# Two prompt tiles loaded channel-major, in an eight-core streaming encoder layer

## The chip, the cores and the metric

The kernel runs on one Trainium2 chip, as one program on all 8 cores, with no exchange between them. The time is the device time of the slowest core in microseconds (us). A core has the engines PE (TensorE: matmuls, and transposes as matmuls), DVE (VectorE), ACT (ScalarE), POOL (GpSimd) and SP (SyncE, which here only starts DMAs). POOL and ACT start DMAs too.

## What is computed

One encoder layer for two groups of rows. The work is split so that each core has 2048 prompt rows (four tiles of 512 rows) and 32 rows of running streams ("sample rows"). Each sub-layer is `x + rmsnorm(f(rmsnorm(x)))`:

```
proj = rmsnorm(x) @ w_in                      # 1024 -> 2048: u | B | C | h, 512 each
y_pool = per group of 128: mean over a trailing window (2, 4, 8, 16) - u, @ w_pool, * scale
y_conv = B * conv3(C * h)                     # causal, depthwise
x = x + rmsnorm(concat(norm_g(y_pool), norm_g(y_conv)) @ w_out)
k, v = rmsnorm(mem) @ w_k, rmsnorm(mem) @ w_v # 256 memory rows; sample rows: cached k, v
x = x + rmsnorm(softmax(rmsnorm(x) @ w_q @ k.T / 16) @ v @ w_co)      # 4 heads of 256
x = x + rmsnorm(relu(rmsnorm(x) @ w_up) ** 2 @ w_down)                # 4096 hidden
rmsnorm(x) = x * rsqrt(mean(x * x, over 1024 channels) + eps) * gain
```

## The kernel before

Matmuls run in bf16 with f32 sums. The contraction index must lie on the partitions, so every projection wants its input channel-major: `xT[0]` and `xT[1]` hold eight slices (`kc`) of 128 channels by 512 rows. The residual `X` is kept row-major, 128 rows by 1024 channels a block, four blocks a tile.

`pre_sub` (line 798) makes a part of `xT` from one block: ACT squares it and sums (`ss`), `rstd` takes `Ln` and `Exp`, `scale_rows` scales the rows into the bf16 buffer `xs` (on DVE or ACT), PE transposes eight 128x128 pieces, and DVE multiplies them from PSUM by the gain, 1024 columns at once. `pre_tile` does that for the four blocks of a tile. Tile 0 is an exception: it is loaded channel-major as f32 (`xt0`) and normed by another path.

The stages, in the order of the program: mixer projections of tiles 0 and 1 (`pool_group`, `conv_group`), `mix_out(0)` and `mix_out(1)` (`out_tile` with `wout`: 16 matmuls of 512 columns for each block), the mixer of tiles 2 and 3 with the four kv blocks (`kv_block`: keys and values of the memory, 16 matmuls each, weights in `wkv`), the fold of keys and values into `Am` and `Bm` (`fold_a`, `fold_b`), attention for all tiles, and the MLP tile by tile. In the MLP `w_up` is streamed in eight blocks through the three buffers `up`, and `w_down` lies in the eight buffers `wdn`, the last four of which are requested when block 7 of `up` has landed. The sample rows go along: `smp_q` (their queries) and `up_smp` (their hidden units) use the weights as the stationary side, with 32 columns moving; `out_smp` uses 32 columns of the sample rows as the stationary side, with 256 weight columns moving and four column groups of the array.

Nothing of this order is written out by hand. Every operation goes into a list with its reads and writes, `Prog.add` finds its dependencies (a tracker of rectangles in SBUF), and `Prog.schedule` replays the list with costs (`c_act`, `c_dve`, `DMA_GBS`, `DMA_FIX`) and takes, for each engine, the ready operation that stands earliest in the program. What comes out is a fixed order for each engine; on the chip each engine goes through its own in order and waits at semaphores. A DMA that POOL starts thus holds up what follows on POOL until its buffer is free. Loads from POOL's queue can convert f32 to bf16; `X` blocks are stored and loaded by SP, which also takes its entries in order.

Of the kernel before, what the change touches and what calls it, by code (L numbers as in the profile page):

```python
# [15 lines left out]
D = 1024  # L16
TP = 2048
# [178 lines left out]
class Prog:  # L196
# [9 lines left out]
    def add(self, opts, reads=(), writes=(), nbytes=0, lead=0, after=None, desc=4096):  # L206

        op = Op()
        op.idx = len(self.ops)
        op.opts = opts  # L210
        op.is_dma = nbytes > 0
        op.bytes = nbytes
        op.desc = desc
        op.deps = {} if after is None else {after: "raw"}
        op.prio = op.idx - lead
        op.ps_new = []
        op.ps_acc = set()
        op.eng = None
        self.ops.append(op)
        multi = len(opts) > 1  # L220
        eng = None if (op.is_dma or multi) else opts[0][0]

        def dep(p, kind):
            if p is not None and p is not op and op.deps.get(p) != "raw":
                op.deps[p] = kind
        for ap in list(reads) + list(writes):
            if isinstance(ap, PV):
                op.ps_acc.add(ap.ps)
                if ap.ps.id not in self.ps_seen:
# [12 lines left out]
        for ap in writes:
            sp, rects = rects_of(ap)
            for r in rects:
                for rec in list(self.tr.find(sp, r)):
                    dep(rec.writer, "war")
                    for rd in rec.readers:
                        dep(rd, "war")
                    q = rec.rect
                    if r[0] <= q[0] and r[1] >= q[1] and r[2] <= q[2] and r[3] >= q[3]:  # L250
                        rec.dead = True
                self.tr.put(sp, r, op)
        return op


    LAT = {("pe", "x"): 0.33, ("x", "pe"): 0.45, ("x", "x"): 0.16, ("s", "s"): 0.10}
    DMA_GBS = {2048: 280.0, 4096: 330.0, 8192: 340.0, 12288: 345.0, 16384: 345.0}
    DMA_FIX = 2.6

    def schedule(self):  # L260
# [14 lines left out]
            if op.ndep == 0:  # L275
                release(op)

        free = {e: 3.5 if e == "pool" else 0.6 for e in self.ENGS}
        hold = {e: 0.0 for e in self.ENGS}
        bank_free = [0.0] * 8  # L280
        bank_busy = [None] * 8
# [3 lines left out]
            for ps in op.ps_acc:  # L285
                ps_left[ps] = ps_left.get(ps, 0) + 1
        dq = {e: [] for e in self.ENGS}
        dq_t = [0.0]

        def dma_next():  # L290
            act = [e for e in self.ENGS if dq[e]]
# [243 lines left out]
def build_program():  # L535
# [4 lines left out]
    def din(name, shape):  # L540
        return nc.dram_tensor(name, list(shape), F32, kind="ExternalInput")
# [1 line left out]
    def dout(name, shape):  # L543
        return nc.dram_tensor(name, list(shape), F32, kind="ExternalOutput")

    xp = din("xp", [TP, D]); xt0 = din("xt0", [4, 128, 1024]); xe = din("xe", [NX, D])
    spool = din("spool", [32, 512]); sconv = din("sconv", [4, 512])
    ckT = din("ckT", [8, 128, 512]); cv = din("cv", [8, 128, 512]); mem = din("mem", [256, D])
    consts = din("consts", [128, 248])
# [2 lines left out]
    gd = {n: din(n, [1, D]) for n in gnames}  # L552
    win_d = din("w_in", [7, 128, 4096])
    wout_d = din("w_out", [128, 8192]); wco_d = din("w_co", [128, 8192])
    wk_d = din("w_k", [16, 128, 512]); wv_d = din("w_v", [16, 128, 512])
    wq_d = din("w_q", [16, 128, 512]); wqT_d = din("w_qT", [16, 128, 512])
    wup_d = din("w_up", [8, 128, 4096]); wdn_d = din("w_down", [8, 128, 4096])
    wpool_d = din("w_pool", [128, 512])
# [76 lines left out]
    sq = rot("sq", 2, TN, BF16)  # L635
    rf = rot("rf", 2, TN)
    mT = rot("mT", 1, 8 * 256, BF16)[0]
    W0 = roff[0]
    assert W0 >= A0 + 106 * K
    wkv = [at("wkv%d" % i, W0 + i * 8192, 4096, BF16) for i in range(2)]  # L640
# [127 lines left out]
        return st[0:r, a:a + n]  # L768


    load(cst[:, :], consts[:, :], 126976, q="act")
    memset(epsb[:, :], EPS)
    act(stat(128), epsb[:, 0:1], AF.Square)
    copy(idb[:, :], idf[:, :])
# [483 lines left out]
    def attn_head(t, hh):  # L1258
# [16 lines left out]
            tt(p2, p2, r.unsqueeze(1).to_broadcast([128, 2, TN]), ALU.mult)  # L1275
        return finish

    def smp_loads():
        wload(kTs[:, :], ckT, 0, 8)
        wload(vSs[:, :], cv, 0, 8)  # L1280

    def smp_q():
        ps = PS(1)
        for j in range(8):
            for kc in range(8):
                mm(ps.v(0, 128, j * NS, (j + 1) * NS), wqk(j, kc), xTek(0, NS)(kc), kc == 0, kc == 7)
# [53 lines left out]
    def up_smp(k, ps):  # L1340
        s = up_slot[(0, k)]
        for jj in range(4):
            c = k * 4 + jj
            cl = c % 16
# [75 lines left out]
    out_smp(lambda kc: mgs[:, kc * NS:(kc + 1) * NS], 8, wo)  # L1420
    pre_tile(2, 0, xT[0])
    mix_out(1)
    for t in range(2, NT):
        for g in range(4):
            step(pool_group(t, g))
            if t == 2:
                kv_done = kv_block(g)
                if g == 0:
                    ext_state_out(kv_done)
                if g < 2:  # L1430
                    kv_loads(g + 2)
# [12 lines left out]
        mix_out(t)
# [176 lines left out]
```

How the kernel before makes its waits and increments, by code:

```python
        def run(e, eng):  # L474
            seen = {}
            ends = sorted(dma_last.items(), key=lambda kv: kv[1].end)
            for n, op in enumerate(seqs[e]):
                if e == "sp" and n == len(seqs[e]) - 1:
                    for k, last in ends:
                        if last.end < op.start - SETTLED and seen.get(k, 0) < last.semval:
                            eng.wait_ge(dsem[k], last.semval)
                            seen[k] = last.semval
                waits = {}
                for p in plan[op]:
                    k, v = (p.sem, p.semval) if p.is_dma else (p.eng, p.sigval)
                    if seen.get(k, 0) >= v:
                        continue
                    if waits.get(k, 0) < v:
                        waits[k] = v
                for k, v in waits.items():
                    eng.wait_ge(dsem[k] if isinstance(k, tuple) else esem[k], v)
                    seen[k] = v
                ins = op.fn(eng, lambda x: x.resolve(psum) if isinstance(x, PV) else x)
                if op.is_dma:
                    ins.then_inc(dsem[op.sem], 16)
                elif op.needs_signal:
                    ins.then_inc(esem[e], 1)
            if e == "sp":
                for k, last in ends:
                    if seen.get(k, 0) < last.semval:
                        eng.wait_ge(dsem[k], last.semval)
```

## Time and profile before

| what | value |
|---|---|
| time, median of 3 runs | 848.71 us (848.17 to 849.42) |
| time of the profiled execution | 848.66 us |
| span of its slowest core (core 6) | 847.1 us |
| PE busy | 813.7 us, 4708 matmuls |
| DVE, ACT, POOL busy | 391.1, 390.8, 102.2 us |
| moved by DMA | 102.39 MB |

The span runs from the first to the last instruction of the slowest core; 1.6 us of the execution lie outside it. The page also has a line with the clock that TensorE was granted in 40 slices; all of them are 9 (90% or more of 2.4 GHz). Matmuls are pipelined: a matmul of 512 columns shows as 0.38 us, but the next one starts 0.22 us after it.

### The profile page before, as it was taken

How to read it: one execution, taken by the hardware profiler on the slowest of the kernel's cores; microseconds unless marked ns; L12 is line 12 of the kernel's file. 1: busy time of each engine (PE TensorE's matmuls, PEld its weight loads, DVE VectorE, ACT ScalarE, POOL GpSimd, SP SyncE). 2: the span in 40 equal slices, each digit the busy share in tenths (PEclk: the TensorE clock that was granted, in tenths of full speed). 3: DMA queues.
4: the chain of work that ended last, by engine and by line, in shares of the span. 5: the costliest groups of instructions: out<-in, count | busy, mean ns of one | idle time of the engine just before them, and what ended most of it. 6: DMA issues, size and time to landing. Idle time of an engine off the chain costs nothing.

```text
span 847.1 us, 13900 instructions; the slowest of 8 cores (841.2 to 847.1 us)
## 1 busy us (share of the span) xinstructions
PE 813.7 (96%) x4708; PEld 391.2 (46%) x4708; DVE 391.1 (46%) x540; ACT 390.8 (46%) x806; POOL 102.2 (12%) x179
## 2 busy tenths in 40 slices
PE   3889999899999999999999999999999999999997
PEld 1444454444644454455454454444444444444443
DVE  4886885568966666765222222241222321222112
ACT  3586786758867556675332233332233411233101
POOL 7612103002111113110010000000000000000000
PEclk9999999999999999999999999999999999999999
DMA  9999439550396606993889716881248820185011
GB/s 196 199 229 202 129 117 208 111 81 1 65 149 113 199 26 187 161 174 84 149 144 165 186 72 132 154 147 53 99 96 156 156 68 26 50 150 100 1 50 50
DMA packets 29793, 102.39 MB, mean 121 GB/s; under 512 B 2386, under 2 KB 13266, under 8 KB 24348
## 3 DMA queue, kind: packets, MB, share of 16 engines
q0 software_dynamic: 19408, 67.32, 46.4%
q1 hardware_dynamic: 9740, 32.75, 11.5%
q10 hardware_dynamic: 576, 1.44, 0.5%
q8 instruction: 39, 0.64, 0.3%
q14 instruction: 30, 0.25, 0.1%
HBM read 144.38 MB, written 18.07 MB: 192 GB/s over the span
## 4 chain that ended last, share of the span: by engine, by line
PE 83%; DMA 11%; DVE 2%; issue 2%; POOL 1%; ACT 1%; another core or an unknown queue 0%; DVEq 0%; ACTq 0%; POOLq 0%
PE ps L670 80%; DMA X<-xp 4%; DMA wdn<-w_down 4%; PE ps L675 2%; DMA wkv<-w_v 2%; DMA up<-w_up 1%; POOL win L744 0%; DVE X L725 0%; ACT junk L699 0%; POOL wdn L744 0%; DVE O L706 0%; DVE z L725 0%; DVE z L706 0%; DVE V L706 0%
## 5 line engine op out<-in xcount | busy, mean ns | idle before, releaser
L670 PE MATMUL ps<-wdn,hid 128*128 128x512 bf16 x1024 | 222.3, 379 | 0.7 <-DMA wdn<-w_down 0.7
L670 PE MATMUL ps<-xT,up 128*128 128x512 bf16 x1024 | 222.6, 379 | 0.0
L670 PEld LDWEIGHTS ps<-wdn,hid 128*128 128x128 bf16 x1024 | 99.9, 98 | 120.4 <-issue 1.2
L670 PEld LDWEIGHTS ps<-xT,up 128*128 128x128 bf16 x1024 | 99.7, 98 | 119.1 <-issue 0.2
L706 DVE TENSOR_TENSOR O<-ps,gp 128x1024 f32<-128x1024 f32 (+1 forms) x49 | 58.3, 1200 | 191.0 <-PE ps L670 122.0
L699 ACT ACTIVATE rt<-ps 128x512 bf16<-128x512 f32 x128 | 76.4, 597 | 142.2 <-PE ps L670 138.3
L670 PE MATMUL ps<-xT,win 128*128 128x512 bf16 x512 | 122.1, 384 | 13.5 <-DMA win<-w_in 12.6
L706 DVE TENSOR_TENSOR hid<-rt 128x512 bf16<-128x512 bf16 x128 | 54.4, 425 | 157.8 <-ACT rt L699 156.0
L699 ACT ACTIVATE sqj<-ps 128x1024 bf16<-128x1024 f32 (+1 forms) x33 | 32.8, 994 | 173.2 <-PE ps L670 171.0
L670 PEld LDWEIGHTS ps<-xT,win 128*128 128x128 bf16 x512 | 49.4, 98 | 71.6 <-issue 17.7
L725 DVE SCALAR_TENSOR_TENSOR X<-O,st,X 128x1024 f32<-128x1024 f32 (+1 forms) x49 | 62.8, 1294 | 4.6 <-DVE O L706 3.8
L744 POOL DMA_DIRECT2D up<-w_up x32 | 17.2, 539 | 378.5 <-PE ps L670 364.9
L706 DVE TENSOR_TENSOR xT<-ps,cst 128x1024 bf16<-128x1024 bf16 x44 | 53.1, 1219 | 20.4 <-PE ps L675 20.2
L670 PE MATMUL ps<-wout,mg 128*128 128x512 bf16 x256 | 58.1, 379 | 3.3 <-DMA wout<-w_out 2.6
L699 ACT ACTIVATE xs<-X 128x1024 bf16<-128x1024 f32 x40 | 41.9, 1050 | 35.4 <-DMA X<-x 31.7
L670 PE MATMUL ps<-xT,Am 128*128 128x512 bf16 x256 | 58.3, 379 | 0.0
L670 PE MATMUL ps<-Bm,mg 128*128 128x512 bf16 x256 | 58.2, 379 | 0.0
L670 PEld LDWEIGHTS ps<-wout,mg 128*128 128x128 bf16 x256 | 24.6, 98 | 31.7 <-issue 3.9
L670 PEld LDWEIGHTS ps<-xT,Am 128*128 128x128 bf16 x256 | 24.2, 98 | 28.5 <-issue 1.7
L670 PEld LDWEIGHTS ps<-Bm,mg 128*128 128x128 bf16 x256 | 24.1, 98 | 27.2 <-issue 0.8
L708 POOL TENSOR_TENSOR psm<-mg 128x512 fp32r<-128x512 bf16 x16 | 19.3, 1208 | 108.8 <-ACT st L699 69.5
L675 PEld LDWEIGHTS ps<-idb,xs 128*128 128x128 bf16 (+1 forms) x412 | 26.2, 98 | 10.2 <-issue 2.0
(184 smaller groups left out, 687.1 us busy)
## 6 DMA issues: line engine op xcount, KB each, us to landing
up<-w_up POOLq DMA_DIRECT2D x32, 1024.0 KB, 9.9
x<-X SPq DMA_DIRECT2D x16, 512.0 KB, 4.2
X<-x SPq DMA_DIRECT2D x16, 512.0 KB, 4.5
wdn<-w_down POOLq DMA_DIRECT2D x8, 1024.0 KB, 30.0
yp<-X SPq DMA_DIRECT2D x15, 512.0 KB, 2.7
X<-xp POOLq DMA_DIRECT2D x8, 512.0 KB, 44.5
X<-xp SPq DMA_DIRECT2D x8, 512.0 KB, 4.4
win<-w_in POOLq DMA_DIRECT2D x4, 768.0 KB, 26.9
```

What stands on the lines that cost most here:

```text
L670: P.add([("pe", lambda e, L: e.matmul(L(out), lhsT=lhsT, rhs=rhs, start=start, stop=stop, skip_group_check=True), max(0.03, n * 0.000421 + ...
L675: P.add([("pe", lambda e, L: e.transpose(out=L(out), in_=in_, identity=idn), 0.065 if in_.dtype == BF16 else 0.25)], reads=[in_, idn], wri ...
L699: return e.activation(out=L(out), in_=L(in_), func=func, scale=scale, **kw)
L706: opts.append(("dve", lambda e, L: e.tensor_tensor(out=L(out), in0=L(in0), in1=L(in1), op=op), c_dve(n, per)))
L708: opts.append(("pool", lambda e, L: e.tensor_tensor(out=L(out), in0=L(in0), in1=L(in1), op=op), 0.18 + n * 0.00168))
L725: return P.add([("dve", lambda e, L: e.scalar_tensor_tensor(out=L(out), in0=L(in0), scalar=scalar, in1=L(in1), op0=op0, op1=op1), c_dve(nc ...
L744: return P.add([(q, lambda e, L: e.dma_start(out=out, in_=in_), 0.5 + nbytes / desc * 0.0005 if q == "pool" else 0.43)], reads=[in_] if rd ...
```

## The change

1. Tiles 2 and 3 of the prompt come a second time, channel-major (`xt23`), and are loaded by POOL's queue straight into `xT` as bf16, one transfer of 2 MB (f32) each. The row-major blocks are still loaded, for the residual and the square sums. `pre_turned` norms `xT` in place: the square sums of the four blocks give four columns of row factors, `rb` splits them into three bf16 parts, POOL multiplies the identity by them (`dg`, three times 512 columns), three matmuls with a matrix of ones turn that into a PSUM tile in which every partition has the 512 row factors, and DVE multiplies the eight slices by gain and factors. No transposes, no `scale_rows` for these two tiles.
2. `w_k` and `w_v` are laid out so that one load reads 16 KB pieces instead of 2 KB pieces.
3. `smp_q` and `up_smp` take the form of `out_smp`: 32 matmuls and 128 matmuls of 256 columns. The result is row-major and `turn_blocks` brings it back with two transposes. `up_smp` now works on two blocks of `up` at once.
4. The scheduler's transfer model has other figures (`DMA_GBS`, start times), and a write that covers an earlier record of the tracker only in part now cuts that record. Both change only which order comes out.

```diff
-                    if r[0] <= q[0] and r[1] >= q[1] and r[2] <= q[2] and r[3] >= q[3]:
+                    if r[0] <= q[0] and r[1] >= q[1] and (sp[0] == "S" or r[2] <= q[2] and r[3] >= q[3]):
                         rec.dead = True
+                        for lo, hi in ((q[2], r[2]), (r[3], q[3])):
+                            if lo < hi:
+                                self.tr.put(sp, (q[0], q[1], lo, hi), rec.writer).readers.update(rec.readers)
...
-    DMA_GBS = {2048: 280.0, 4096: 330.0, 8192: 340.0, 12288: 345.0, 16384: 345.0}
+    DMA_GBS = {1024: 150.0, 2048: 275.0, 4096: 310.0, 8192: 325.0, 12288: 325.0, 16384: 328.0}
...
-        free = {e: 3.5 if e == "pool" else 0.6 for e in self.ENGS}
+        free = {e: 6.9 if e == "pool" else 1.0 for e in self.ENGS}
...
-        dq_t = [0.0]
+        dq_t = [2.6]
...
+    def load_turned(t):
+        load(xT[t % 2][:, :], xt23[t - 2], 2097152, q="pool", desc=16384)
+
+    def pre_turned(t):
+        n = NSUB
+        ss, ln, rs, rem = (stat(128, n) for _ in range(4))
+        for i in range(n):
+            act(xsr[xs_n[0] % 2][:, :], Xof[(t, i)], AF.Square, accum=ss[:, i:i + 1])
+            xs_n[0] += 1
+        act(ln, ss, AF.Ln, scale=1.0 / D, bias=epsb[:, 0:1])
+        act(rs, ln, AF.Exp, scale=-0.5)
+        left = rs
+        for q in range(3):
+            b = rb[:, q * n:(q + 1) * n]
+            copy(b, left)
+            if q < 2:
+                tt(rem, left, b, ALU.subtract)
+                left = rem
+        tt(r3(dg[:, :], 3 * n), idb[:, :].unsqueeze(1).to_broadcast([128, 3 * n, 128]),
+           rb[:, :].unsqueeze(2).to_broadcast([128, 3 * n, 128]), ALU.mult, eng="pool")
+        ps = PS(1)
+        for q in range(3):
+            mm(ps.v(0, 128, 0, TN), ones[:, :], dg[:, q * TN:(q + 1) * TN], q == 0, q == 2)
+        for kc in range(8):
+            x = xT[t % 2][:, kc * TN:(kc + 1) * TN]
+            stt(x, x, gcs[:, kc:kc + 1], ps.v(0, 128, 0, TN), ALU.mult, ALU.mult)
...
-        wload(wkv[k % 2][:, :], wk_d if k < 2 else wv_d, 8 * (k % 2), 8 * (k % 2) + 8, after)
+        load(wkv[k % 2][:, :], (wk_d if k < 2 else wv_d)[k % 2], 2097152, q="pool", after=after, desc=16384)
...
+    def turn_blocks(rows, dst):
+        ps = PS(1)
+        for q in range(2):
+            tr(ps.v(0, 128, q * 128, (q + 1) * 128, BF16), rows[:, q * 128:(q + 1) * 128], idb[:, :])
+        copy(dst.rearrange("p (g q t) -> p g q t", g=4, q=2),
...
-        for j in range(8):
-            for kc in range(8):
-                mm(ps.v(0, 128, j * NS, (j + 1) * NS), wqk(j, kc), xTek(0, NS)(kc), kc == 0, kc == 7)
-        copy(qTs[:, :], ps.v(0, 128, 0, 8 * NS), eng="act dve")
+        for kc in range(8):
+            for hh in range(4):
+                w = r3(wq[:, :], 8)[:, 2 * hh:2 * hh + 2, kc * 128:(kc + 1) * 128]
+                mm(ps.v(32 * hh, 32 * hh + 32, 0, 256, F32, lambda a: r3(a, 2)), xTek(0, NS)(kc), w, kc == 0, kc == 7, share=3)
+        q = rts[:, 0:256]
+        copy(q, ps.v(0, 128, 0, 256), eng="act dve")
+        turn_blocks(q, qTs[:, :])
...
-            for kc in range(8):
-                mm(ps.v(0, 128, cl * NS, (cl + 1) * NS), s[:, jj * 1024 + kc * 128: jj * 1024 + (kc + 1) * 128],
-                   xTek(0, NS)(kc), kc == 0, kc == 7)
...
+        for kc in range(8):
+            for g in range(4):
+                w = r3(up_slot[(0, k + g // 2)][:, :], 4)[:, 2 * (g % 2):2 * (g % 2) + 2, kc * 128:(kc + 1) * 128]
+                mm(ps.v(32 * g, 32 * g + 32, 0, 256, F32, lambda a: r3(a, 2)), xTek(0, NS)(kc), w, kc == 0, kc == 7, share=3)
+        r, h = rts[:, 0:256], rts[:, 256:512]
+        act(r, ps.v(0, 128, 0, 256), AF.Relu)
+        tt(h, r, r, ALU.mult, per=0.5)
+        turn_blocks(h, hids[:, k * 128:(k + 2) * 128])
...
         step(conv_group(0, cc))
+    load_turned(2)
     pre_tile(1, 0, xT[1], junk)
...
     step(None)
+    load_turned(3)
     ext_conv_rest()
...
-    pre_tile(2, 0, xT[0])
+    pre_turned(2)
     mix_out(1)
...
             if cc == 1 and t + 1 < NT:
-                pre_tile(t + 1, 0, xT[(t + 1) % 2])
+                pre_turned(t + 1)
...
-            if t == 0:
-                if k % 4 == 0:
-                    ups = PS(1)
-                up_smp(k, ups)
+            if t == 0 and k % 2 == 0:
+                up_smp(k)
```

How the order moves at the start of tile 2. On PE, from the end of `mix_out(1)` (`wout,mg_81`) through kv blocks 0 and 1 (`wkv`, with transposes of `xs`) to the first projections of tile 2 (`xT_54,win`), before:

```order
L670 MATMUL ps<-wout,mg_81 128x512 x21
L670 MATMUL ps<-wkv_111,mT_110 128x512 x10
L675 MATMUL ps<-idb,xs_58 128x128 x8
L670 MATMUL ps<-wkv_111,mT_110 128x512 x6
L675 MATMUL ps<-idb,xs_59 128x128
L670 MATMUL ps<-wkv_112,mT_110 128x512 x5
L670 MATMUL ps<-xT_54,win 128x512 x8
L675 MATMUL ps<-idb,xs_59 128x128 x7
L670 MATMUL ps<-xT_54,win 128x512 x8
L670 MATMUL ps<-wkv_112,mT_110 128x512 x4
```

and now:

```order
L675 MATMUL ps<-wout,mg_81 128x512 x53
L675 MATMUL ps<-wkv_113,mT_110 128x512 x16
L680 MATMUL ps<-idb,xs_59 128x128
L675 MATMUL ps<-wkv_114,mT_110 128x512 x9
L680 MATMUL ps<-idb,xs_59 128x128 x7
L675 MATMUL ps<-wkv_114,mT_110 128x512 x7
L680 MATMUL ps<-idb,xs_58 128x128 x8
L675 MATMUL ps<-dg,ones 128x512 x3
L680 MATMUL ps<-cst,se_72 32x128 x4
L680 MATMUL ps<-cst,se_72 4x128 x2
L675 MATMUL ps<-xT_54,win 128x512
```

Projections of tile 2 stood in the middle of kv block 1; now both kv blocks are through before `dg`, and the first projection comes after it.

On POOL, around the two loads of `w_v` into `wkv`, before:

```order
L737 COPY vh_98<-V_97 128x2
L737 COPY V_97<-vh_98 128x2
L744 DMA wkv_111<-w_v 128x8x512
L708 TENSOR_TENSOR sAB_102<-U_92 128x527
L737 COPY se_72<-Us 128x32
```

and now:

```order
L749 DMA xT_55<-xt 128x4096
L742 COPY vh_98<-V_97 128x2
L742 COPY V_97<-vh_98 128x2
L749 DMA wkv_113<-w_v 128x4096
L713 TENSOR_TENSOR dg<-idb,rb_112 128x1536
L749 DMA wkv_114<-w_v 128x4096
```

The product `dg` stands between the two loads, and the load of tile 3 (`xT_55`) ahead of them.

On SP, the stores of `x1` and the loads of the tiles 2 and 3 after `mix_out(0)` began, before:

```order
L744 DMA x<-X 128x1024
L744 DMA gps<-gs 128x256
L744 DMA X<-xp 128x1024
L744 DMA x<-X 128x1024
L744 DMA X<-xp 128x1024
```

and now:

```order
L749 DMA x<-X 128x1024 x2
L749 DMA X<-xp 128x1024
L749 DMA gps<-gs 128x256
L749 DMA x<-X 128x1024
L749 DMA X<-xp 128x1024
```

The fourth load of tile 2 (the first `X<-xp` before, the last one now) stood right behind tile 0's last store and now has the store of tile 1's first block ahead of it.

## Rows read from the trace of the kernel before

**Rows 1.** The page: the chain that ended last, by engine and by line.
```profile
PE 83%; DMA 11%; DVE 2%; issue 2%; POOL 1%; ACT 1%; another core or an unknown queue 0%; DVEq 0%; ACTq 0%; POOLq 0%
...
PE 813.7 (96%) x4708; PEld 391.2 (46%) x4708; DVE 391.1 (46%) x540; ACT 390.8 (46%) x806; POOL 102.2 (12%) x179
```

**Rows 2.** PE's waits, whole span: for whom, us in total, times, longest.
```profile
PE ps L670 <- DMA win<-w_in: 12.9, 2, 12.6
PE ps L670 <- DMA wout<-w_out: 2.6, 1, 2.6
PE ps L670 <- DMA wkv<-w_v: 2.2, 2, 2.0
...
PE ps L670 <- DVE Am L735: 0.8, 1, 0.8
PE ps L670 <- DMA wdn<-w_down: 0.7, 1, 0.7
```

**Rows 3.** Timeline of PE: start, length, what, count, idle before it.
```profile
300.02 0.67 PE L670 MATMUL ps<-xTe,wq 128*128 128x32 bf16 x20
300.54 0.61 PE L675 MATMUL ps<-idb,xs 128*128 128x128 bf16 x8
300.98 0.61 PE L670 MATMUL ps<-xTe,wq 128*128 128x32 bf16 x18
...
382.98 1.97 PE L670 MATMUL ps<-xTe,up 128*128 128x32 bf16 x72
384.80 20.88 PE L670 MATMUL ps<-xT,up 128*128 128x512 bf16 x96
405.51 0.38 PE L670 MATMUL ps<-xTe,up 128*128 128x32 bf16 x9
...
502.35 3.68 PE L670 MATMUL ps<-wdn,hids 128*32 128x256 bf16 x128
505.96 1.68 PE L670 MATMUL ps<-xT,up 128*128 128x512 bf16 x7
```

**Rows 4.** Timelines of POOL and PE, and the DMA list, at the `wdn` transfers.
```profile
422.29 0.53 POOL L744 DMA_DIRECT2D up<-w_up  x1 [6.89 <-PE ps L670]
...
434.14 0.54 POOL L744 DMA_DIRECT2D wdn<-w_down  x1 [0.51 <-issue]
...
466.00 14.19 PE L670 MATMUL ps<-wdn,hid 128*128 128x512 bf16 x65 [0.73 <-DMA wdn<-w_down]
...
wdn<-w_down POOLq DMA_DIRECT2D x1, 1024.0 KB, 31.7
```

**Rows 5.** Prices for tile 2: groups, DMA landings, DVE's timeline, one stretch.
```profile
L708 POOL TENSOR_TENSOR psm<-mg x16: 1149/1156/1924, 253.2 to 367.8; 128x512 fp32r<-128x512 bf16 x16
L733 ACT ACTIVATE xs<-ps 128x512 bf16<-128x512 f32 x4 | 2.4, 598 | 1.2 <-PE ps L675 1.2
L706 DVE TENSOR_TENSOR O<-ps,gp 128x1024 f32<-128x1024 f32 x47 | 56.9, 1221 | 181.0 <-PE ps L670 122.0 <-ACT sqj L699 46.8 <-ACT st L699 11.4
L725 DVE SCALAR_TENSOR_TENSOR X<-O,st,X x12: 1274/1277/2083, 78.1 to 198.5; 128x1024 f32<-128x1024 f32 x12
DMA to landing us min/median/max: 2.7/4.8/14.7
...
up<-w_up POOLq DMA_DIRECT2D x32, 1024.0 KB, 9.9
wkv<-w_v POOLq DMA_DIRECT2D x2, 1024.0 KB, 19.8
...
107.07 0.74 DVE L725 SCALAR_TENSOR_TENSOR z<-V,cst,z 128x512 f32<-128x512 f32 x1
107.73 0.74 DVE L725 SCALAR_TENSOR_TENSOR mg<-z,cst,rf 128x512 bf16<-128x512 f32 x1
...
124.50:163.00 38.50, 36.20 (x195) 17.16 (x193) 21.64 (x28) 26.71 (x44) 8.62 (x22) 1.00 0.77 175
```

**Rows 6.** Timelines of DVE and POOL in the first tile.
```profile
26.07 0.89 DVE L725 SCALAR_TENSOR_TENSOR ple<-se,Us 128x32 bf16<-128x32 f32 x1 [0.98 <-ACT U L733]
28.23 0.19 DVE L725 SCALAR_TENSOR_TENSOR ple<-se,Us 128x32 bf16<-128x32 f32 x1
...
25.86 1.05 POOL L708 TENSOR_TENSOR sAB<-U 128x527 f32<-128x527 f32 x1
```

More of the change, by code:

```diff
@@ L544, in dout @@
         return nc.dram_tensor(name, list(shape), F32, kind="ExternalOutput")
-    xp = din("xp", [TP, D]); xt0 = din("xt0", [4, 128, 1024]); xe = din("xe", [NX, D])
+    xp = din("xp", [TP, D]); xt0 = din("xt0", [4, 128, 1024]); xt23 = din("xt23", [2, 128, 8 * TN]); xe = din("xe", [NX, D])
     spool = din("spool", [32, 512]); sconv = din("sconv", [4, 512])
@@ L554, in build_program @@
     wout_d = din("w_out", [128, 8192]); wco_d = din("w_co", [128, 8192])
-    wk_d = din("w_k", [16, 128, 512]); wv_d = din("w_v", [16, 128, 512])
+    wk_d = din("w_k", [2, 128, 4096]); wv_d = din("w_v", [2, 128, 4096])
     wq_d = din("w_q", [16, 128, 512]); wqT_d = din("w_qT", [16, 128, 512])
@@ L637, in build_program @@
     mT = rot("mT", 1, 8 * 256, BF16)[0]
+    dg = at("dg", hids.off, 3 * TN, BF16)
+    rb = rot("rb", 1, 3 * NSUB, BF16)[0]
     W0 = roff[0]
@@ L768, in stat @@
         return st[0:r, a:a + n]
-    load(cst[:, :], consts[:, :], 126976, q="act")
+    load(cst[:, :], consts[:, :], 126976, q="act", desc=2048)
     memset(epsb[:, :], EPS)
@@ L1276, in attn_head @@
         return finish
+    def turn_blocks(rows, dst):
[3 more added lines that the diff above has]
+        copy(dst.rearrange("p (g q t) -> p g q t", g=4, q=2),
+             ps.v(0, 128, 0, 256, BF16, lambda a: a.rearrange("p (q g t) -> p g q t", q=2, g=4)), eng="act dve")
     def smp_loads():
@@ L1338, in up_chunk, with up_smp @@
         tt(hid(c), r, r, ALU.mult, per=0.5)
[L1340 to L1344, printed above, removed]
-            for kc in range(8):
-                mm(ps.v(0, 128, cl * NS, (cl + 1) * NS), s[:, jj * 1024 + kc * 128: jj * 1024 + (kc + 1) * 128],
-                   xTek(0, NS)(kc), kc == 0, kc == 7)
-        if k % 4 == 3:
-            act(rts[:, :], ps.v(0, 128, 0, 512), AF.Relu)
-            tt(hids[:, (k // 4) * 512:(k // 4 + 1) * 512], rts[:, :], rts[:, :], ALU.mult, per=0.5)
+    def up_smp(k):
+        ps = PS(1)
+        for kc in range(8):
[6 more added lines that the diff above has]
+        turn_blocks(h, hids[:, k * 128:(k + 2) * 128])
     wd = lambda kc, h: dparts[kc // 4][:, (kc % 4) * D + h * 512: (kc % 4) * D + (h + 1) * 512]
@@ L1479, in build_program @@
     load_gps(2)
-    ups = None
     for t in range(NT):
@@ L1548, in oct, with sides @@
         return f(a.reshape(128, 8, 4096).transpose(1, 0, 2))
+    def sides(w):
+        return f(chunks(f(w).reshape(D, D), 512).reshape(128, 2, 4096).transpose(1, 0, 2))
     def blk(a):
@@ L1558 @@
         "w_out": f(rows(w_out[0])).reshape(128, -1),
-        "w_k": blk(chunks(f(w_k[0]).reshape(D, D), 512)), "w_v": blk(chunks(f(w_v[0]).reshape(D, D), 512)),
+        "w_k": sides(w_k[0]), "w_v": sides(w_v[0]),
         "w_q": blk(chunks(f(w_q[0]).reshape(D, D), 128)),
@@ L1585 @@
         d["xt0"] = halves(x_prompt[b, t0:t0 + TN])
+        d["xt23"] = f(x_prompt[b, t0 + 2 * TN:t0 + 4 * TN].reshape(2, TN, 8, 128).transpose(0, 3, 2, 1).reshape(2, 128, 8 * TN))
         halo = f(x_prompt[b, t0 - XH:t0]) if half == 1 else np.zeros((XH, D), np.float32)
```

## The prediction

> **What bounds the kernel now.** I read the page first: its busy line and its chain that ended last. PE is busy for 96% of the span, and the chain runs through PE's matmul line for 80% of it [rows 1]. The clock row on the page shows nines throughout, so the granted clock is the 2.4 GHz level all along and no term comes from it. Then PE's waits [rows 2]: all of them together are some 14 us, of which 12.9 us are the wait for the first weights, up to 12.64 us. The others are small, and those that the change touches are 2.6 us for `wout`, 2.2 us for `w_v`, 0.8 us for `Am` and 0.7 us for `wdn`. So the time is PE's work plus a few short waits. A microsecond of PE work that goes is a microsecond of time, unless PE then stands before something that comes no earlier. Two such places stand in the trace: PE reaches `wout` 2.6 us too early (near 60 us), and it reaches the last `wdn` transfer 0.7 us too early (466 us) [rows 2, 4]. What is saved ahead of either is lost at it. The profiled execution took 848.66 us with a span of 847.1 us; the median of the runs is 848.71 us, so nothing is to be converted.
>
> **Transposes of tiles 2 and 3.** Eight 128-column transposes take PE 0.44 us (300.54 to 300.98) [rows 3], 0.055 us each. 64 of them go: 3.5 us. Six 512-column matmuls on `dg` come: PE walks 96 such matmuls in 20.71 us [rows 3], 0.216 us each, so 1.3 us. Net **-2.2 us**. On DVE four PSUM multiplies of 1.22 us and its share of the row scalings per tile are exchanged for eight of 0.74 us; neither DVE nor ACT is the bound over these stretches, and I price that at nothing except where the chain below says otherwise.
>
> **The sample rows.** Before, 20 matmuls of 32 columns take 0.52 us [rows 3], 0.026 us each, and `smp_q` has 64: 1.7 us. The new form is that of `out_smp` (a 32-column stationary, 256 moving columns, four column groups): 128 of them take 3.61 us [rows 3], 0.028 us each. 32 of them and two transposes make 1.0 us: **-0.7 us**. `up_smp` had 87 of its 256 matmuls ahead of the first wide `up` matmul (384.80 us), 2.2 us at 0.0253 (72 in 1.82 us) [rows 3]; now 32 stand there, 0.9 us: **-1.3 us**. Behind 384.80 us there were 169 of them, 4.3 us, and now there are 96 and eight transposes, 3.1 us: 1.2 us less work, which I count at **nothing**. The reason is the `wdn` chain. Before, the slot for `up` block 7 is asked for at 422.29 us, the last `wdn` is issued at 434.14 us and lands 31.7 us later, and PE waits for it until 466.00 us [rows 4]. The block's slot comes free when block 4 and the sample work that reads it are through: five blocks and 73 small matmuls (1.86 us) before, five blocks and 64 of the new form with four transposes (2.0 us) now, because `up_smp` takes two blocks at a time. So the transfers start at the same distance from 384.80 us as before, the last `wdn` lands at the same distance, and PE comes to it 1.2 us sooner and waits about 2 us instead of 0.7.
>
> **The start.** The order on POOL's queue is the same up to `wout`, so `wout` lands near 60 us as before. Eight more transposes of tile 1 stand ahead of the first `wout` matmul; they fall into its 2.6 us wait: **-0.4 us**.
>
> Work together: 2.2 + 0.7 + 1.3 + 0.4 = **4.6 us** less.
>
> **What comes back at tile 2.** This is the uncertain part. `pre_turned` makes one serial chain out of four independent ones: the square sums of all four row blocks, `Ln` and `Exp`, five tiny DVE operations, one POOL product of 1536 columns, three matmuls, then eight DVE products, and only then projections. I walk it from 110 us, where PE is in `mix_out(0)` in both. The last row block's load now stands on SP behind the store of tile 1's first block. That store waits for its residual; by 3.5 us of matmuls, a square, a multiply of 1.22 and a residual of 1.28 us [rows 5] it goes at about 119.6 us, the load lands near 125 us (4.8 us, the median) [rows 5], and its square is done at 126. On ACT and DVE the chain then stands behind the evacuation of `mix_out(1)`'s last block: `Exp` at about 128.6, the third `rb` cast at about 132, since a residual of 1.28 us is in front of it. POOL: the nearest row is the 512-column `psm` product at 1.16 us [rows 5], three times that is 3.5 us (bounds 3.3 and 5), so `dg` is there at 135.5. PE meanwhile has `mix_out(1)` to 126.1, two kv blocks of 3.5 us and their transposes, and waits about 1.0 us for the ACT cast (0.60 us) [rows 5] ahead of the last eight transposes, since no other work is queued there now. It stands at `dg` from 135.0: 0.6 us more. Then the first product: 0.38 us of pipeline and 0.74 us on DVE, less 0.65 us of small state transposes, 0.6 us. After that the ramp holds: DVE brings a 128-row slice every 0.66 us (107.07 to 107.73) [rows 5], and three pool groups are interleaved, 0.65 us of PE work a slice; 0.35 us for the second slice. `w_v` is issued at about 130.7 us, when kv block 0 has been read, and PE asks for it at about 141. With 16 KB pieces an `up` load of this size lands in 9.9 us, `w_v` in 2 KB pieces took 19.8 us [rows 5], with SP's row loads beside it. I take 12 us, nearer to the first: 1.2 us of wait. Sum 3.75 us, against 2.2 us of `w_v` waits that go: **+1.55 us**. Bounds: -2.2 us (PE never stands there) to +5.5 us (POOL at 5 us, `w_v` at 15 us).
>
> **Tile 3.** The second `dg` product has a whole `mix_out` behind it for its eight products. What it may cost is a lock: DVE's 32-column `ple` product took 0.89 us while POOL's `sAB` ran (25.86 to 26.91 us) and ended with it, and 0.19 us with POOL idle [rows 6]. In the new order two `z` products follow the last `rb` cast on DVE, and one of them can sit out the 3.5 us. PE has 36 matmuls (7.8 us) before it needs that chain, which is about 9 us long then. **+0.5 us**, between 0 and 3.5. The Trainium skill says the same more generally ("SBUF — State Buffer", "Who interferes with whom": a VectorE instruction with two SBUF inputs contends with a GpSimd instruction that reads SBUF, and whoever issues first holds the pair for its whole length). By that rule the `z` product waits out all of `dg`; the rows agree for the short case, and it is a rival below. The in-place products of tiles 2 and 3 read one of their inputs from PSUM, and by that rule they are not held.
>
> **The fold.** `mix_out(3)` now runs ahead of the 64 fold matmuls, not behind them, so PE no longer stands before it for `Am` copies: **-0.8 us** [rows 2]. Other short waits (0.2 to 1.1 us each) I leave as they are.
>
> Sum: -4.6 + 1.55 + 0.5 - 0.8 = -3.35 us, 848.66 - 3.35 = **845.3 us**.
>
> **Where it covers itself.** `load_turned(2)` is issued near 56 us and queues behind transfers that land by 87 us, then 7 us of its own; DVE asks for it at 136. `load_turned(3)` goes at 103.5 and is asked for at 190. On POOL each blocks only halo copies that are due after it. `w_v`'s first load now stands ahead of `dg` on POOL and waits for kv block 0 (130.7), before `dg` is ready (132).
>
> **Rivals.**
> 1. *PE is not held at tile 2.* If the chain is 2 us shorter than walked (the row load in 3.5 us, quicker casts) and `w_v` lands in 10 us, three of the terms go (0.6 + 0.6 + 1.2): 842.9 us. For it: the projections of three groups are interleaved slice by slice. Against: nothing else is queued for PE between 126 and 137 us. 0.20.
> 2. *The lock counts in full.* `dg` holds DVE's `z` product for its whole length and PE has nothing in its place: 845.3 - 0.5 + 3.5 = 848.3 us, no change. 0.14.
> 3. *Slower: tile 2's last row load is late.* The chain has 1.7 us of slack up to its square; everything later delays every projection of tile 2. A row load has taken up to 14.7 us [rows 5], when it ran beside `w_v`. At that price the square is done 10 us later, PE stands 8.3 us more: 853.6 us. It decides from 7 us of delay (slower than 850.4). Against: POOL's queue has nothing to move between 114 and 130 us. 0.10.
> 4. *The saved work is real, but moved waits of the new order eat it* (the stretch from 60 to 110 us is re-sorted too): 848.0 to 849.5 us. 0.06.
>
> The forecast itself has 0.50. About 0.2% (1.7 us) is what a measurement of this kernel can tell from no change. Faster by more (under 847.0): the forecast and rival 1, 0.70. Within: rivals 2 and 4, 0.20. Slower (over 850.4): 0.10. The range leaves out rival 3 and a little at either end: 842.3 to 849.0 us.
>
> **What would show it.** PE's count falls by 208 matmuls and its busy time by about 5 us. PE's idle time from 124.5 to 163 us, 2.3 us before (38.50 less 36.20) [rows 5], should be 3 to 4.5 us, put down to ACT, POOL `dg` and DVE `xT`. The wait for `wdn` should be near 2 us. If it stays under 1 us, my chain there is wrong, and `up_smp` pays in full. `dg` should take 3.3 to 5 us, the product `xT` 0.74 us. The forecast fails if PE's wait near `dg` is over 5 us, or if waits of over 1 us stand where none did from 60 to 110 us.

## The result, and the profile after

The change makes the kernel slower. The median is 854.2 us against 848.65 us for the kernel before on the same chip, and the ratio of the two is 1.0059, 95% interval 1.0047 to 1.0071. (One of the six runs, 1011 us with one half of the chip at a lower clock, is in the median of 854.2 but left out of the ratio; the median of the other five is 853.8.) The forecast was 845.3 us, 842.3 to 849.0.

From the page of the kernel after, whose lines answer to those in [rows 1]: span, busy times, clock in 40 slices, and the chain that ended last.

```profile
span 850.9 us, 13491 instructions; the slowest of 8 cores (844.0 to 850.9 us)
PE 815.9 (96%) x4500; PEld 385.7 (45%) x4500; DVE 396.9 (47%) x562; ACT 382.8 (45%) x792; POOL 104.9 (12%) x182
PEclk9899999999989999999999999999999999999999
PE ps L675 85%; DMA wdn<-w_down 4%; PE ps L680 2%; DMA wkv<-w_v 2%; DMA XT<-xt 1%; DMA up<-w_up 1%; DMA pool_p<-sT 1%; DVE sqx L711 1%; ACT sqx L704 0%; POOL sAB L713 0%; ACT sq L704 0%; DVE O L711 0%; POOL se L713 0%; DVE X L730 0%; POOL wdn L749 0%
```

PE has 208 matmuls fewer, as forecast, yet it is busy 2.2 us longer (815.9 against 813.7), not 5 us shorter. Two slices of the clock row are an 8, the second in the start and the twelfth (234 to 255 us) at the place told below, and a 32 KB store of state, `pool_p`, stands in the chain. PE's waits, which answer to [rows 2] (releaser: us in total, times, longest):

```profile
PE ps L675 <- DMA win<-w_in: 12.7, 1, 12.7
PE ps L675 <- ACT sq L704: 5.5, 3, 4.3
PE ps L675 <- DMA wkv<-w_v: 2.6, 1, 2.6
PE ps L680 <- ACT xs L721: 1.8, 2, 1.1
...
PE ps L675 <- DVE xT L720: 0.4, 1, 0.4
...
PE ps L675 <- POOL dg L713: 0.4, 1, 0.4
```

The new entry that counts is the second: one wait of 4.3 us for ACT. PE's timeline at the end of tile 3's mixer shows its place (start, us, then in brackets the idle time before and its releaser):

```profile
227.09 3.69 PE L675 MATMUL ps<-wout,mg 128*128 128x512 bf16 x16
235.11 0.58 PE L675 MATMUL ps<-sq,bd 128*128 128x512 bf16 x1 [4.33 <-ACT sq L704]
235.49 11.60 PE L675 MATMUL ps<-wout,mg 128*128 128x512 bf16 x41
246.93 2.35 PE L675 MATMUL ps<-kT,wqT 128*128 128x256 bf16 x20
```

`mix_out(3)` does 16 matmuls and then stands before the square `sq` of the last convolution group. ACT's timeline says why that square is late:

```profile
224.81 0.59 ACT L738 ACTIVATE sT<-ps 16x512 f32<-16x512 f32 x1 [1.84 <-PE ps L680]
...
227.80 0.63 ACT L704 ACTIVATE rf<-rf 128x512 f32<-128x512 f32 x1
233.73 0.59 ACT L738 ACTIVATE sT<-ps 2x512 f32<-2x512 f32 x1 [5.29 <-DMA pool_p<-sT]
234.34 0.63 ACT L704 ACTIVATE sq<-z 128x512 bf16<-128x512 f32 x1
```

ACT sits 5.3 us before a copy of two rows of state, until `pool_p` has landed (issued at 225.47 us, 8.2 us to landing, beside the load of `wco`), and `sq` is queued behind. The two transfers have nothing to do with each other: the copy writes rows 32 and 33 of `sT`, the store reads rows 0 to 15. But `sT` lies in the memory of `hids`, and the change puts `dg` there too, as 128 rows. The tracker's record of `dg` covers all the rows. The store's read is noted at it, and the copy, which overlaps the same record, must wait for its readers. Before, no record of 128 rows was there, and the copy ran right behind the instruction ahead of it (ACT, core 6 of before):

```profile
227.91 0.59 ACT L733 ACTIVATE sT<-ps 2x512 f32<-2x512 f32 x1
```

Then the 41 matmuls take 11.6 us, 0.28 us each, where the pace is 0.22. The windows of the same core (stretch, its length, PE busy and matmuls, clock) show it, and the same stretches for e1 below:

```profile
220.00:231.00 11.00, 10.56 (x64) 1.00 0.34 56
231.00:235.00 4.00, 0.00 (x0) 0.86 1.15 164
235.00:242.00 7.00, 6.89 (x20) 0.59 0.86 127
242.00:247.00 5.00, 5.00 (x25) 1.00 1.11 147
```

From 235 to 242 us the mean granted clock is 0.59 of 2.4 GHz, so most of it ran at the 1.2 GHz level, and 20 matmuls were done. A stretch of this kind is in the records of seven of the eight cores, and it begins in or right behind this wait (2.3 to 4.3 us). The slow cores are those with the long wait:

```profile
core 0: 845.0 us, clock 0.996
core 1: 850.9 us, clock 0.988
core 2: 849.9 us, clock 0.994
core 3: 844.6 us, clock 0.994
core 4: 850.6 us, clock 0.996
core 5: 844.0 us, clock 0.996
core 6: 844.0 us, clock 0.994
core 7: 848.9 us, clock 0.992
```

Cores 1, 2, 4 and 7 waited 4.3, 4.0, 4.2 and 3.9 us; cores 0, 3, 5 and 6 waited 2.4, 2.9, 2.4 and 2.3, and core 0 is the one that kept the full clock. The length of the wait goes with the store: `pool_p` took 7.7 to 8.2 us to land on the four slow cores and 6.2 to 6.7 us on the other four.

Stage by stage, worked out from the timelines, as means over the eight cores of each trace in us (the last column is e1, below, on another chip):

| from / to | before | after | e1 |
|---|---|---|---|
| first projection to first kv block | 110.3 | 109.1 | 109.8 |
| to the first attention matmul (`xT,Am`) | 121.0 | 128.6 | 123.9 |
| to the first wide `up` matmul | 136.8 | 133.8 | 134.1 |
| to the end | 461.9 | 462.0 | 461.5 |

Six `wco,vT` matmuls (1.3 us) moved from the third stretch to the second. The loss is all in the second: 7.7 us, of which 4.8 are gone in e1. (These are means over cores; the time is that of the slowest core, where the long waits add up, so its figures below are larger.) The 2.9 us that stay in e1 hold the 1.3 us that only moved and what tile 2 costs. There, too, the clock falls on some cores: in the kernel after, cores 0, 1, 2 and 7 have a stretch at 1.2 GHz between 134 and 146 us, behind waits for `xs` and `dg` (0.8 and 1.1 to 1.5 us) or for `w_v` (2.6 us); in the trace of before there is none in this part.

### The profile page after: what moved, and what is told of

Same layout as the page of the kernel before. It is cut to its first block, busy times and chain, and to the rows that moved or that the text cites. A ratio compares the mean times of both kernels' runs of the same rounds, so it can differ in the third digit from the quotient of the medians.

```text
span 850.9 us, 13491 instructions; the slowest of 8 cores (844.0 to 850.9 us)
## 1 busy us (share of the span) xinstructions
PE 815.9 (96%) x4500; PEld 385.7 (45%) x4500; DVE 396.9 (47%) x562; ACT 382.8 (45%) x792; POOL 104.9 (12%) x182
## 4 chain that ended last, share of the span: by engine, by line
PE 87%; DMA 8%; ACT 1%; issue 1%; DVE 1%; POOL 1%; ACTq 0%; POOLq 0%; DVEq 0%; SPq 0%
PE ps L675 85%; DMA wdn<-w_down 4%; PE ps L680 2%; DMA wkv<-w_v 2%; DMA XT<-xt 1%; DMA up<-w_up 1%; DMA pool_p<-sT 1%; DVE sqx L711 1%; ACT sqx L704 0%; POOL sAB L713 0%; ACT sq L704 0%; DVE O L711 0%; POOL se L713 0%; DVE X L730 0%; POOL wdn L749 0%
## 5 line engine op out<-in xcount | busy, mean ns | idle before, releaser
L675 PE MATMUL ps<-xT,win 128*128 128x512 bf16 x512 | 125.9, 392 | 14.6 <-DMA win<-w_in 12.7
L675 PE MATMUL ps<-wout,mg 128*128 128x512 bf16 x256 | 60.2, 391 | 0.0
L711 DVE TENSOR_TENSOR xT<-ps,cst 128x1024 bf16<-128x1024 bf16 x36 | 43.4, 1219 | 18.2 <-PE ps L680 18.2
L680 PE MATMUL ps<-idb,xs 128*128 128x128 bf16 (+1 forms) x348 | 25.9, 218 | 3.3 <-ACT xs L721 1.8
```

What stands on the lines that cost most here:

```text
L675: P.add([("pe", lambda e, L: e.matmul(L(out), lhsT=lhsT, rhs=rhs, start=start, stop=stop, skip_group_check=True), max(0.03, n * 0.000421 + ...
L680: P.add([("pe", lambda e, L: e.transpose(out=L(out), in_=in_, identity=idn), 0.065 if in_.dtype == BF16 else 0.25)], reads=[in_, idn], wri ...
L711: opts.append(("dve", lambda e, L: e.tensor_tensor(out=L(out), in0=L(in0), in1=L(in1), op=op), c_dve(n, per)))
```

## Experiments

**Theories.** A: ACT's wait for `pool_p`, and the half clock behind it, is the loss. B: it is the serial chain of tile 2. M: it is the re-sorted order of the new transfer model. The kernel before took 848.5 to 852.1 us on the chips of these runs, so I go by ratios to it, measured side by side.

**The wait taken away.** The 2x512 copy gets a buffer of its own, `sTc` (memory of `sAB`, free by then). ACT's order differs by one place, nothing else.

```diff
+    sTc = at("sTc", sAB[0].off, 512, rows=2)
...
-        copy(sT[32:34, :], ps.v(0, 2, 0, 512), eng="act")
-        dma("sp", o_conv_p[:, :], sT[32:34, :], 4096, wr=False)
+        copy(sTc[0:2, :], ps.v(0, 2, 0, 512), eng="act")
+        dma("sp", o_conv_p[:, :], sTc[0:2, :], 4096, wr=False)
```

> The changed kernel (854.2 us) with one edit: the second state output of tile 3 (2x512) is written to a buffer of its own, not to the one that shares memory with dg, so ACT does not wait for the transfer pool_p to land. The order of all engines stays as it is but for that copy, one place earlier. Theory A (this wait and what follows it is the loss): PE's wait of 2.3 to 4.3 us on sq in mix_out(3) falls under 0.5 us, the stretch of half clock behind it goes where it follows the wait, and the time is 847 to 849. Theory B (the serial chain of tile 2 is the loss): 852 to 854, as PE still stands the same at tile 2. Theory M (the re-sorted start is the loss): 851 to 854.

Measured: 0.9973 (0.9956 to 0.9989), 846.4 us on the scale of 848.65. ACT's and PE's timelines of e1, its slowest core (1), and the windows of PE:

```profile
229.18 0.57 ACT L738 ACTIVATE sTc<-ps 2x512 f32<-2x512 f32 x1
...
231.26 0.63 ACT L704 ACTIVATE sq<-z 128x512 bf16<-128x512 f32 x1 [1.00 <-DVE z L711]
```

```profile
232.03 0.38 PE L675 MATMUL ps<-sq,bd 128*128 128x512 bf16 x1
232.25 9.23 PE L675 MATMUL ps<-wout,mg 128*128 128x512 bf16 x42
```

```profile
231.00:235.00 4.00, 4.00 (x19) 1.00 0.81 143
235.00:242.00 7.00, 7.00 (x38) 1.00 0.98 151
```

No wait, full clock, 38 matmuls where there were 20. Because the chips differ I ran the pair again beside each other, the changed kernel unchanged and with this edit.

> The changed kernel, unchanged, on the same chip as the next three: ratio 1.004 to 1.007, half clock at the end of the mixer of tile 3 on most cores.

> The kernel of e1_state_own again, beside the changed kernel. Theory A: 0.006 to 0.009 under f1_changed_again.

Measured: 1.0049 (1.0031 to 1.0067) and 0.9964 (0.9951 to 0.9976): 0.0085, or 7.2 us, for two rows of state in the wrong place. PE, core 2 of each (in f1 it waited 3.3 us), 225 to 250 us, f1 first:

```profile
225.00:250.00 25.00, 21.48 (x96) 0.86 0.75 119
```

```profile
225.00:250.00 25.00, 24.45 (x150) 1.00 0.89 134
```

**The wait put into the kernel before.** Each engine's order stays; the one dependency is added after scheduling.

```diff
+        store = dma("sp", o_pool_p[:, :], sT[0:16, :], 32768, wr=False)
...
+        held.append((copy(sT[32:34, :], ps.v(0, 2, 0, 512), eng="act"), store))
...
+    P.schedule(); held[0][0].deps[held[0][1]] = "war"
```

> The kernel before, every engine's order untouched, with one wait added: the 2x512 state copy on ACT waits until pool_p has landed. Theory A: ACT stands 5 us, its Am copies and the square of the last convolution group are queued behind, PE stands 3 to 5 us in the fold, and half clock follows on several cores: ratio 1.004 to 1.009. If the wait in itself is harmless and it was the new order around it that cost, 0.999 to 1.002.

Measured: 1.0051 (1.0035 to 1.0068), 4.3 us from one wait. ACT, then PE, of its core 1:

```profile
231.16 0.59 ACT L733 ACTIVATE sT<-ps 2x512 f32<-2x512 f32 x1 [4.77 <-DMA pool_p<-sT]
231.78 0.63 ACT L699 ACTIVATE rf<-rf 128x512 f32<-128x512 f32 x1
232.31 2.04 ACT L733 ACTIVATE Am<-ps 128x512 bf16<-128x512 f32 x4
```

```profile
225.69 1.91 PE L670 MATMUL ps<-kT,wqT 128*128 128x256 bf16 x16
231.90 4.42 PE L670 MATMUL ps<-kT,wqT 128*128 128x256 bf16 x20 [4.29 <-ACT sT L733]
```

Here the fold stands there, and it is held as well: its results leave PSUM through `Am` copies on ACT, which are queued behind. PE waited 2.1 to 4.3 us, and on seven of eight cores the clock fell to half at it or right behind it. Theory A holds from both sides: the wait taken away gives the time back, and the wait alone, put into the kernel before, costs it.

**Does the fold cover the wait?** The changed kernel with the fold emitted ahead of the state copies:

```diff
         if t == NT - 1:
+            for c in range(8): fold_a(c)
             state_out()
...
-    for c in range(8):
-        fold_a(c)
```

> The changed kernel with the fold of keys (64 matmuls) emitted ahead of the state outputs and mix_out(3), as it ran before; ACT still waits for pool_p ahead of the 2x512 state copy. Theory A (the wait on ACT is what costs, and only because PE has nothing left there): ACT's wait of some 5 us stays, PE loses 0 to 2 us at it instead of 2.3 to 4.3, and the ratio is 0.997 to 1.000. If it stays at 1.004 or above, the order of the fold is not what exposes the wait.

Measured: 1.0023 (1.0010 to 1.0037), between the two outcomes named, and a miss of the 0.997 to 1.000. PE no longer waits in `mix_out(3)`. But ACT, core 0, stands longer, and PE meets it at the next thing that needs ACT, the first row block of the attention:

```profile
243.97 0.59 ACT L738 ACTIVATE sT<-ps 2x512 f32<-2x512 f32 x1 [7.51 <-DMA pool_p<-sT]
```

```profile
252.09 1.01 PE L680 MATMUL ps<-idb,xs 128*128 128x128 bf16 x8 [3.46 <-DVE xs L720]
```

My claim that the order exposes the wait was half right: the fold covers it in the mixer, and then PE stands 3.0 to 3.5 us at this place on four cores, three of them with a stretch at 1.2 GHz behind it, and 1.2 to 1.7 us on the others.

**The tiles the old way.** `load_turned` out, `pre_tile` for `pre_turned`, all else as changed; and tile 3 alone channel-major, with the state buffer of e1.

```diff
-    pre_turned(2)
+    pre_tile(2, 0, xT[0])
...
-                pre_turned(t + 1)
+                pre_tile(t + 1, 0, xT[(t + 1) % 2])
```

> The changed kernel with tiles 2 and 3 made the old way (row-major, scaled, transposed), all else as changed (sample rows, w_k and w_v in 16 KB pieces, transfer model, tracker). No dg, so no wait of the state output on pool_p. Theory A: 848 to 850, as the 2.2 us of transposes come back and the wait at mix_out(3) goes. Theory B: 845 to 847. Theory M: 851 to 854, as the start is the same as in the changed kernel.

> The kernel of e1_state_own with tile 2 made the old way and tile 3 alone channel-major. Theory C (tile 3's share is a clean 1.1 us of PE work, tile 2's serial chain gives its 1.1 us back and more): ratio 0.9955, some 1.5 us under e1_state_own and 1.1 us under e2_no_turned (0.9966). If tile 3 brings nothing either: 0.9966 to 0.9973.

Measured: e2 0.9966 (0.9952 to 0.9980), e7 0.9950 (0.9936 to 0.9964). e2 is at 845.8 us on the scale of 848.65, theory B's figure, and under the 848 to 850 that A gave it. But it has neither the chain nor the false wait, and e1, which keeps the chain, comes to the same place. So the wait is the loss, B falls as its cause, and A's 2.2 us for the transposes were wrong: with `w_v` where it is, the channel-major tiles are worth nothing together, tile 3 alone perhaps 1.4 us (e7 against e2), within the intervals.

**More time for `w_v`.** PE waited for `w_v` 0.7 to 2.6 us in e1 and 2.5 to 4.1 us in e7. `kv_block` 2 and 3 go behind the first two convolution groups of tile 2: on e1 (e6, again as f3), on e7 (e8), and on e2 (e11, again as f4).

```diff
-            if t == 2:
+            if t == 2 and g < 2:
...
             step(conv_group(t, cc))
+            if t == 2 and cc < 2:
+                kv_block(2 + cc)
```

> The kernel of e1_state_own with the two value blocks of the memory (kv_block 2 and 3) emitted behind the first two convolution groups of tile 2, not between its pool groups, so that w_v has some 10 us more to land. Theory W (what eats the gain of the turned tiles is the wait for w_v, 0.7 to 2.6 us, and the half clock that follows it on some cores): no wait for w_v, and 1.5 to 3 us less than e1_state_own, ratio 0.994 to 0.996. If the waits only move (xT slices not there yet): ratio 0.997.

> e7_turn3_only (tile 3 alone channel-major, own state buffer) with kv_block 2 and 3 behind the first two convolution groups of tile 2. PE waited 2.5 to 4.1 us for w_v in e7; if nothing takes the place of that wait, 2 to 3 us under e7, ratio 0.992 to 0.993. If the projections of tile 2 only meet their xT slices instead, as in e6, 0.9945 to 0.996.

> e2_no_turned (both tiles made the old way) with kv_block 2 and 3 behind the first two convolution groups. w_v waits of 2.4 to 3.5 us in e2 go: ratio 0.993 to 0.995. Against e8 it tells what tile 3 channel-major is worth once w_v is no bound: 1.1 us (0.0013).

> The kernel of e6_kv_later again (both tiles channel-major, own state buffer, value blocks later). If the channel-major tiles pay once w_v is no bound, it is at or under f4_rows_kv_later; if their serial chain costs PE as much as 64 transposes, as e6 and e11 say from two chips (0.9969 and 0.9941), it is 0.002 to 0.003 above.

> The kernel of e11_no_turn_kv_later again (both tiles row-major and transposed, value blocks later), the fastest so far: 0.993 to 0.996.

| | tiles | ratio |
|---|---|---|
| e6 / f3 | both channel-major | 0.9969 (0.9950 to 0.9988) / 0.9984 (0.9973 to 0.9996) |
| e8 | tile 3 alone | 0.9973 (0.9960 to 0.9986) |
| e11 / f4 | both row-major | 0.9941 (0.9927 to 0.9954) / 0.9929 (0.9907 to 0.9952) |

The waits for `w_v` are gone in all of them, but only the row-major version turns that into time. e6 missed its 0.994 to 0.996 and is where it was to be if the waits only move; e8 missed both of its ranges and is not even under e7. e8 and e11 shared a chip: tile 3 channel-major costs 0.0032 there, 2.7 us, where I had expected it to give 1.1. f3 and f4 shared another: the two channel-major tiles cost 0.0055, 4.7 us, twice what I had expected and in spite of 2.2 us less PE work. The windows of PE from the first kv block to the attention, f3 core 6 and then f4 core 7, two cores at full clock there (they show 3.5 us of the difference as waits):

```profile
123.10:173.50 50.40, 48.29 (x242) 1.00 0.69 152
173.50:246.30 72.80, 70.26 (x378) 1.00 0.40 61
```

```profile
124.40:171.90 47.50, 47.42 (x276) 1.00 0.80 166
171.90:245.00 73.10, 72.06 (x400) 1.00 0.41 63
```

PE stands 4.7 us in f3 (50.40 - 48.29 and 72.80 - 70.26) and 1.1 us in f4. In f3 these are small waits: `sq` 1.4, `xs` 0.8, `rf` 0.7, `dg` 0.4. I infer that the transposes, which PE can do between, cover such waits in f4; I did not test it. **The kernel of e11 and f4 is the fastest**: 0.6 to 0.7% under the one before, without the channel-major tiles.

**The other parts alone**, each in the kernel before: the sample rows, the model with the tracker's cut, and `w_k`, `w_v` in 16 KB pieces. Their diffs are those of the change.

> The kernel before with smp_q and up_smp in the new form alone; the order up to the attention is that of before. By the sum on record 0.7 + 1.3 us = 2.0 us faster (846.7), with 2 us of wait for wdn. If the wait for wdn stays under 1 us, up_smp pays in full and it is 3.2 us faster (845.5). If the sample rows are part of the loss, it is at 848.7 or above.

> The kernel before with the new transfer model and the tracker cut alone: the same work in another order. Theory M: 2 us or more slower (851 or above), with new waits ahead of 110 us. Theories A and B: 848 to 850, since neither the chain of tile 2 nor the wait on pool_p is in it.

> The kernel before with w_k and w_v laid out for 16 KB pieces alone. In the trace of before PE waited for w_v on three cores of eight (0.3 to 2.2 us). Theory: these waits go and nothing else, ratio 0.998 to 1.000. If the faster load is worth more than its waits, under 0.998.

> The kernel before, unchanged, for a trace from the same chip as the next three: ratio 1.000, no wait of over 1 us at the end of the mixer of tile 3, and no stretch of half clock there on any core, by every theory.

Measured: e3 0.9983 (0.9969 to 0.9997), 1.4 us where 2.0 was the sum, with up to 2.2 us of wait for `wdn`; e4 1.0007 (0.9990 to 1.0024), e9 1.0051 (1.0037 to 1.0064), the kernel before against itself 0.9989 (0.9970 to 1.0007). e4 rules out theory M as the main loss. e9 missed its expectation widely. The transfers land sooner, yet PE waits more. The issue rows (KB each, median us to landing) of before and of e9, then PE's wait in e9's slowest core:

```profile
wkv<-w_v POOLq DMA_DIRECT2D x2, 1024.0 KB, 19.8
```

```profile
wkv<-w_v POOLq DMA_DIRECT2D x2, 1024.0 KB, 13.7
```

```profile
PE ps L670 <- DMA wkv<-w_v: 4.8, 2, 2.8
```

The planner prices 16 KB pieces at 345 GB/s with 2.6 us fixed, 8.7 us for 2 MB, where 2 KB pieces cost it 10.1 us, and it places the matmuls by that. PE stood 1.9 to 4.8 us on the eight cores, where it was 0 to 2.2 us before. And the clock goes with it: on cores 1 to 5, behind waits for `w_v` of 2.2 to 3.3 us, there is a stretch at 1.2 GHz between 144 and 149 us, on core 7 one behind a wait of 2.8 us at 154, and the trace of before has none there. Core 3 of e9:

```profile
144.00:148.00 4.00, 4.00 (x11) 0.57 1.05 171
```

So e9 looks like the main loss again, with another wait in front; I ran nothing that takes that wait out of e9. On top, `mix_out(3)` stands ahead of the fold in e9 too. The three parts alone add to +0.0041, but together (e2) they give -0.0034: each run is a new order, and the effects of such parts do not add. Which places make up that difference I have not settled.

## Why the prediction was wrong, point by point

- **The fold is the step that failed: its -0.8 us, and the sentence behind it, "Other short waits (0.2 to 1.1 us each) I leave as they are".** "PE no longer stands before it for `Am` copies" is right: that wait is gone. But the sum put every new wait on `mix_out(3)` at nothing, without a look at what ACT's queue ahead of it waits for. A wait of 5.3 us on ACT came in its place, with 2.3 to 4.3 us of it on PE. The old order would not have saved it: with the fold at that place (e10) the same wait costs 4.3 us of time. It could have been seen: the code has `dg` at the offset of `hids`, where `sT` lies. None of the rivals was this mechanism; rival 4 ("moved waits") had its kind at 848 to 849.5 us and 0.06.
- **"No term comes from it", said of the clock,** failed with it. A PE that waits some us and then runs at 1.2 GHz pays again: f1 against f2 is 7.2 us for a wait of at most 4.0 us. The nines were those of core 6 alone; in the same trace five other cores (0, 2, 3, 4 and 5) have a stretch at 1.2 GHz near 40 us, behind four waits of 0.3 to 1.0 us.
- **PE's waits before, "some 14 us".** A slip in the reading: the five rows of [rows 2] alone add to 19.2 us, and all waits listed for that core to 27.3. No term hangs on it.
- **Transposes (-2.2 us) and sample rows (-0.7, -1.3 us).** The work went, in count as forecast. From the first attention matmul to the first wide `up` matmul 3.0 us went, 1.7 without the six that moved, against 2.0 forecast. The sample rows alone (e3) gave 1.4 us.
- **`up_smp` behind 384.8 us, counted at nothing.** From the first wide `up` matmul to the end nothing changed (461.9 and 462.0 us as means), so the total was near. One core makes that mean: core 4 of after waited 2.5 us for `wdn`, ran at 1.2 GHz behind it and took 465.5 us; the other seven have 461.5 as their mean. The reason that I gave was not shown: the wait for `wdn` was 0.2 us on the slowest core, not 2 us, and 0 to 2.5 us over the eight. By my own sign my chain is wrong there: block 7 was asked for 37.8 us behind the first wide matmul (37.5 before), as I had it, but the last `wdn` went out at 48.4 us, not 49.3.
- **The start (-0.4 us).** Not there. The stretch up to the kv blocks is 1.2 us shorter, which is the 24 transposes of tile 2 that left it (1.3 us). The 2.6 us wait for `wout` stood on core 6 of before alone (0.3 us on core 0). PE now waits 1.8 us for `xs` of tile 1 (1.1 us at 61 us, 0.6 at 63).
- **Tile 2 (+1.55 us).** Idle from 124.5 to 163 us was 4.1 us (38.50 less 34.37), inside the 3 to 4.5 forecast: 0.8 for the cast (1.0 forecast), 0.4 for `dg` (0.6), 2.6 for `w_v` (1.2). `w_v` took 15.4 us, over my upper end of 15; the product `dg` took 2.74 and 3.12 us, under my lower end of 3.3. That the total came out is in part luck: the terms were off both ways.
- **Tile 3's lock (+0.5 us).** The mechanism is there, the price is not. POOL and DVE, core 1:

```profile
172.24 3.12 POOL L713 TENSOR_TENSOR dg<-idb,rb 128x1536 bf16<-128x1536 bf16 x1 [0.77 <-DVE rb L740]
```

```profile
172.00 3.91 DVE L730 SCALAR_TENSOR_TENSOR z<-V,cst,z 128x512 f32<-128x512 f32 x2
177.69 0.73 DVE L730 SCALAR_TENSOR_TENSOR xT<-xT,cst,ps 128x512 bf16<-128x512 bf16 x1
```

Two `z` products, 0.75 us each elsewhere, took 3.9 us: the second took 3.05 us of them and ended 0.5 us behind `dg`. The trace agrees here with the sentence of the Trainium skill that I weighed ("SBUF — State Buffer", "Who interferes with whom"), and in full length. PE had other matmuls in its queue and waited 0.2 us at most.

With the false wait away, e1 and f2 come to 846.4 and 845.6 us (0.9973 and 0.9964 of 848.65). The sum of 845.3 us was about right for the kernel that I thought I saw, as a whole and not term by term. Its terms for the two tiles (-2.2, +1.55, +0.5) leave -0.15 us, and e1 against e2 says +0.6, within the intervals; the rest of it (-0.7, -1.3, -0.4, -0.8) leaves -3.2, and e2 measured 2.9 us less than before, though the start gave nothing.

## What to carry to other kernels

Where a new buffer is laid over old memory, look at every wait that this adds, also on small copies: an engine that takes its work in order passes a wait for a 32 KB store on to all that is queued behind it. When one such wait ends in dense matmul work, count the slower clock behind it too. And a saving on the bounding engine is worth nothing until one knows what it will stand before, so measure parts in the order in which they will run, not one by one.

## What the runs showed of the hardware that I had not expected

- Waits of 2.1 to 4.3 us of PE in the middle of dense work went with a stretch at 1.2 GHz, at their end or right behind them, on 20 of 24 cores (changed kernel twice, e10). In the fourteen traces without a wait at that place there was no such stretch there on any core. It is not certain: in f1, core 6 waited 3.7 us and kept the full clock. Nor is it bound to this place or to one long wait: in the kernel before run again (b0), cores 5, 6 and 7 waited 2.3 to 2.9 us before `mix_out(0)` and have such a stretch behind it (the other five waited 1.6 to 2.2 us and have none), and the stretches near 40 us stand behind four waits of 0.3 to 1.0 us. The Trainium skill ("TensorE: Matmul & The Clock Gate", "HAM oscillation — how this bites in real kernels") describes waits within the work that send the array back to the lower clock; these rows agree with it in kind.
- The 32 KB store `pool_p` took 5.6 to 9.7 us to land over all cores and traces; in the kernel after it was 6.2 to 8.2, and the slow cores were those with the long ones.
- The 2 MB loads of `w_v` (figures are a core's median of two) landed in 13.0 to 13.7 us in 16 KB pieces (e9) and in 16.2 to 18.7 us in 2 KB pieces (e10), on one chip. Over all traces it was 12.5 to 17.1 and 14.7 to 20.2 us.
